# Last chunk's output rows: squares of the first halves ahead, two half rows scaled by ScalarE and GpSimd, VectorE's closing order written out

## The reference, cut to what matters

```python
    x = x + merged @ w_o[l].astype(merged.dtype)
    return rmsnorm(x, final_g)

def rmsnorm(x, g, eps=NORM_EPS):
    xf = x.astype(jnp.float32)
    y = xf * lax.rsqrt(jnp.mean(xf * xf, axis=-1, keepdims=True) + eps)
    return (y * g.astype(jnp.float32)).astype(x.dtype)
```

## Time and profile before

| | us |
|---|---|
| median of 3 runs | 2284.22 (2283.36 to 2284.63) |
| the profiled execution | 2282.93 |
| its span, first to last instruction | 2281.1 |
| TensorE busy | 2257.2 (99% of the span) |
| VectorE busy | 1426.0 (63%) |
| ScalarE busy | 756.0 (33%) |
| GpSimd busy | 232.8 (10%) |

### The profile page before, as it was taken

The page is one execution under the profiler, slowest core; times in us unless marked ns, Lnnn a source line. Parts: engine busy times, 40 slices in busy tenths (PEclk is TensorE's granted clock), DMA queues, the critical chain, the costliest instruction groups (busy, mean ns, idle before and its releaser), DMA issues.

```text
span 2281.1 us, 29046 instructions
## 1 busy us (share of the span) xinstructions
PE 2257.2 (99%) x10822; PEld 1832.9 (80%) x10822; DVE 1426.0 (63%) x2706; ACT 756.0 (33%) x1610; POOL 232.8 (10%) x186
## 2 busy tenths in 40 slices
PE   7999999999999999999999999999999999999998
PEld 6888888878888888888788788888877787788886
DVE  4767667764666665564557667665556657677752
ACT  4333332342333331032344344102135455441121
POOL 3544400100000000010000000001000000000010
PEclk9999999999999999999999999999999999999999
DMA  8877788798566665566755565556765555545555
GB/s 315 288 265 265 270 289 290 273 342 321 166 203 183 181 175 183 190 254 238 263 185 170 166 199 156 169 196 239 257 258 144 179 161 168 156 136 183 187 193 201
DMA packets 99339, 493.53 MB, mean 216 GB/s; under 512 B 15360, under 2 KB 18304, under 8 KB 54144
## 3 DMA queue, kind: packets, MB, share of 16 engines
q1 hardware_dynamic: 90464, 488.90, 63.8%
q10 hardware_dynamic: 8736, 2.78, 0.6%
HBM read 378.37 MB, written 113.27 MB: 216 GB/s over the span
## 4 chain that ended last, share of the span: by engine, by line
PE 96%; DVE 2%; DMA 1%; issue 1%; ACT 0%; SPq 0%; DVEq 0%; ACTq 0%
PE PJ L769 75%; PE SC L828 6%; PE SC L860 5%; PE TB L869 3%; PE OB L893 1%; PE OB L894 1%; PE OB L828 1%; PE PJ L828 1%; PE OB L896 1%; PE OB L895 1%; PE TB L904 0%; DMA Wraw<-w_stream 0%; DMA PX<-x_t 0%; PE TB L920 0%; PE SC L769 0%
## 5 line engine op out<-in xcount | busy, mean ns | idle before, releaser
L769 PE MATMUL PJ<-hT,Wp 128*128 128x512 f32 x6480 | 1571.4, 394 | 0.5 <-DVE PX L1632 0.5
L769 PEld LDWEIGHTS PJ<-hT,Wp 128*128 128x128 f32 x6480 | 1189.5, 188 | 254.0 <-issue 17.7
L1552 DVE SCALAR_TENSOR_TENSOR ACCS<-UA,col,ACCS 128x512 f32<-128x512 f32 x464 | 350.7, 798 | 0.4
L1066 ACT ACTIVATE PX<-SC,negm 128x512 f32<-128x512 f32 (+3 forms) x320 | 196.2, 623 | 145.5 <-DVE negm L1381 143.6
L1426 DVE TENSOR_TENSOR ZA<-TB,ZA 128x512 fp32r<-128x512 f32 (+1 forms) x144 | 95.1, 660 | 177.0 <-ACT ZA L1086 176.0
L1381 DVE TENSOR_REDUCE negm<-SC 128x2 f32<-128x1024 f32 (+3 forms) x160 | 169.0, 1061 | 40.3 <-PE SC L860 37.6
L1086 ACT ACTIVATE ZA<-TB 128x512 fp32r<-128x512 f32 (+1 forms) x144 | 82.6, 574 | 321.8 <-PE TB L869 321.8
L1137 ACT ACTIVATE TG<-PJ,col 128x512 f32<-128x512 f32 x64 | 44.1, 690 | 351.2 <-PE PJ L769 351.2
L1419 DVE SCALAR_TENSOR_TENSOR PX<-PX,sc 128x512 f32<-128x512 f32 (+3 forms) x160 | 108.0, 695 | 51.0 <-ACT PX L1077 50.8
L828 PE MATMUL SC<-Wp,KM 128*128 128x512 f32 x384 | 121.5, 389 | 0.0
L1077 ACT ACTIVATE PX<-PX,sc 128x512 f32<-128x512 f32 (+3 forms) x160 | 98.9, 655 | 64.9 <-DVE sc L1408 44.6
(11 more groups left out here) (192 smaller groups left out, 2037.4 us busy)
## 6 DMA issues: line engine op xcount, KB each, us to landing
Wp<-split_weights SPq DMA_DIRECT2D x264, 1024.0 KB, 4.8
split_weights<-Wp SPq DMA_DIRECT2D x88, 1024.0 KB, 4.9
Wraw<-w_stream SPq DMA_DIRECT2D x88, 512.0 KB, 5.9
KM<-keys SPq DMA_DIRECT2D x24, 512.0 KB, 5.9
VM<-values SPq DMA_DIRECT2D x24, 512.0 KB, 6.5
PX<-x SPq DMA_DIRECT2D x16, 512.0 KB, 7.6
out<-PX SPq DMA_DIRECT2D x16, 512.0 KB, 10.6
keys<-KM SPq DMA_DIRECT2D x12, 512.0 KB, 9.5
```

The costliest lines, as they stand in the source:

```text
L769: mm = pe.matmul(pj(c, r)[:, :], wt, rhs[:, 1 if q == 1 else 0, k, :], start=(n == 0), stop=(n == 3 * ktiles - 1))
L1066: a = act.activation(probs(c, h, t, j, m)[:, 0:w], SC[k][:, m, 0:w], ACT.Exp, bias=negm[:, t % 2, j, m:m + 1], accum_out=lsum[:, t % 2, j, ...
L1552: a = dve.scalar_tensor_tensor(out=acc, in0=src, scalar=col[:, n:n + 1], in1=acc, op0=ALU.mult, op1=ALU.add)
```

## The change

Only the last chunk is touched. ScalarE squares the first halves of the four rows ahead, while TensorE works on half 1, into `xst[:, 0, t]`; after the end of the projection it squares only the second halves, and VectorE adds the two sums, with one more 128x1 instruction ahead of each clamp. For rows 0 and 1, VectorE scales only the second half. The first half is multiplied by the factor on ScalarE (`end_scale`) and by `ffull` on GpSimd (`end_half`), and the stores of these two rows wait for both. VectorE's order at the end is written out, and so are ScalarE's and GpSimd's.

```diff
             def store_rows(c, t):
                 sp.wait_ge(row_ready, NT * c + t + 1)
+                if c == NCHUNK - 1 and t < 2:
+                    sp.wait_ge(half_ready, t + 1)
...
+            def half_square(t):
+                act.wait_ge(fin_freed, 8 * (NCHUNK - 1) + t + 1)
+                wait(act, half_squared, t)
+                if t == 0:
+                    act.wait_ge(rsq_done, NT * (NCHUNK - 1))
+                act.activation(junk[:, 0:CHUNK], xres[:, t, 0:CHUNK], ACT.Square, accum_out=xst[:, 0, t:t + 1]
+                               ).then_inc(half_squared, 1)
...
+                        if c == NCHUNK - 1 and p == FIN_AT + 26 + t:
+                            half_square(t)
...
-            for t in range(NT):
-                row_square(NCHUNK - 1, t)
+            def end_square(t):
+                act.wait_ge(fin_freed, 8 * (NCHUNK - 1) + NT + t + 1)
+                act.wait_ge(rsq_done, NT * (NCHUNK - 1) + t)
+                if t == 0:
+                    act.wait_ge(half_squared, NT)
+                act.activation(junk[:, 0:CHUNK], xres[:, t, CHUNK:], ACT.Square, accum_out=rst[:, 0, t:t + 1]).then_inc(rsq_done, 1)
+
+            def end_scale(t):
+                act.wait_ge(scale_ready, t + 1)
+                act.activation(xres[:, t, 0:CHUNK], xres[:, t, 0:CHUNK], ACT.Copy, scale=rst[:, 5, t:t + 1]).then_inc(half_scaled, 1)
+
+            end_square(0)
+            end_square(1)
+            end_square(2)
+            end_scale(0)
+            end_square(3)
+            end_scale(1)
...
-            for t in range(NT):
-                row_power(NCHUNK - 1, t)
+            def end_half(t):
+                pool.wait_ge(half_scaled, t + 1)
+                pool.tensor_tensor(xres[:, t, 0:CHUNK], xres[:, t, 0:CHUNK], ffull[:, 0:CHUNK], ALU.mult).then_inc(half_ready, 1)
+
+            row_power(NCHUNK - 1, 0)
+            row_power(NCHUNK - 1, 1)
+            end_half(0)
+            row_power(NCHUNK - 1, 2)
+            row_power(NCHUNK - 1, 3)
+            end_half(1)
...
-            for n in range(NT + 2):
-                if n < NT:
-                    add_rows(NCHUNK - 1, 1, n)
-                if n > 0 and n <= NT:
-                    row_clamp(NCHUNK - 1, n - 1)
-                if n > 1:
-                    row_scale(NCHUNK - 1, n - 2)
+            def end_clamp(t):
+                dve.wait_ge(rsq_done, NT * (NCHUNK - 1) + t + 1)
+                dve.wait_ge(half_squared, t + 1)
+                step(dve.tensor_tensor(rst[:, 0, t:t + 1], rst[:, 0, t:t + 1], xst[:, 0, t:t + 1], ALU.add))
+                clamp(rst, t, rvar_ready)
+
+            def end_rows(t):
+                n = NT * (NCHUNK - 1) + t
+                if t == 0:
+                    dve.wait_ge(f_loaded, 16 * NCHUNK)
+                dve.wait_ge(rpow_done, n + 1)
+                dve.wait_ge(rvar_ready, n + 1)
+                dve.tensor_tensor(rst[:, 5, t:t + 1], rst[:, 4, t:t + 1], rst[:, 3, t:t + 1], ALU.mult).then_inc(scale_ready, 1)
+                dve.wait_ge(scale_ready, t + 1)
+                first = CHUNK if t < 2 else 0
+                dve.scalar_tensor_tensor(out=xres[:, t, first:], in0=xres[:, t, first:], scalar=rst[:, 5, t:t + 1],
+                                         in1=ffull[:, first:], op0=ALU.mult, op1=ALU.mult).then_inc(row_ready, 1)
+
+            add_rows(NCHUNK - 1, 1, 0)
+            add_rows(NCHUNK - 1, 1, 1)
+            end_clamp(0)
+            add_rows(NCHUNK - 1, 1, 2)
+            end_clamp(1)
+            end_rows(0)
+            add_rows(NCHUNK - 1, 1, 3)
+            end_clamp(2)
+            end_rows(1)
+            end_clamp(3)
+            end_rows(2)
+            end_rows(3)
```

More of the change, by code:

```diff
@@ L542, in build @@
             sem("rsq_done"), sem("rvar_ready"), sem("rpow_done"), sem("row_ready"))
+        half_squared, scale_ready, half_scaled, half_ready = (
+            sem("half_squared"), sem("scale_ready"), sem("half_scaled"), sem("half_ready"))
         const_pool = sem("const_pool")
```

## The result

The changed kernel takes 2286.61 us (median of 22 runs, 2285.37 to 2288.25) against 2283.86 us for the kernel before (22 runs, 2282.78 to 2284.84) measured beside it: 2.75 us more, a ratio of 1.0012 (95% interval 1.0007 to 1.0018). That is within the 0.2% that was set as no change, and on the slow side of it. The interval, +1.6 to +4.1 us, holds the forecast (+2.57; 2286.8 us) and also rival D (+3.95); which of them it was, the profile has to tell.

The account below looks back on a forecast made before the run. VectorE's queue, then the last store, bound the end. Row 3's scaling: -0.66 + 0.91 + 1.09 = +1.34 us; with three stores in a row the span's end moves +2.57: 2284.22 + 2.57 = 2286.8 us, range 2283.5 to 2288.2.

Parts of the forecast that it names:

- rival D: At row 2's scaling VectorE wins the SBUF access and GpSimd's second half row comes later: +3.95 us, 2288.2 us; chance 0.10.
- What bounds: Behind the last matmul, VectorE's queue and then the last store set the end, not ScalarE's squares; 9.5 us cap any gain.
- The squares and sums: Half squares on ScalarE win nothing; VectorE's extra 128x1 sums cost three steps of 0.18 us on the path, +0.54 us.
- Half scaling: VectorE's scaling of rows 0 and 1 falls to 128x512, 0.60 us less each, a gain of 1.20 us.
- VectorE's own account: VectorE's gain from half scaling less its extra sums, before any hold: -1.20 + 0.54 = -0.66 us.
- The holds: GpSimd's two products hold VectorE at row 2's sum, +0.91 us, and at row 3's L1665, +1.09 us.
- The one that waits goes first: At SBUF access, the engine already waiting is served next: GpSimd's second product starts at 2276.78, ahead of row 3's L1665.
- The stores: Stores 2 and 3 queue behind store 1, which waits for GpSimd; three pass in a row at 1.28 us each.
- A: Rival: GpSimd's product doesn't hold VectorE, but the stores bunch at the end: +1.1 us, 2285.3 us; chance 0.15.
- B: Rival: VectorE is held but stores overlap, so the last row alone counts: +1.3 us, 2285.5 us; chance 0.12.
- C: Rival: neither holds nor bunched stores, VectorE's -0.66 us goes straight to the end: 2283.6 us; chance 0.08.
- D with a product of 1.9 us: Rival D with GpSimd's product at 1.9 us instead of 1.29: claimed over the bound of measurement; 0.04 left to slower.

## Why the prediction was right, point by point

- **What bounds.** VectorE's queue and then the last store, not ScalarE's squares: shown by the version with whole rows on VectorE, where all squares are halved and the tail is longer.
- **The squares and sums.** +0.54 us was forecast, +0.59 measured in row 3's readiness; a step is 0.19 and not 0.18 us. The half squares run from 2251.24 to 2254.42 and ScalarE is then idle for 14.51 us, so their cover held.
- **Half scaling.** The forecast took 0.60 us off for each of two rows; it is 0.53. The short scaling with these operands lasts 0.75 us and moves the next start by 0.67, where the row that was used, L1611 in the earlier trace rows, had 0.69. VectorE's own account is -0.48 and not -0.66 us. The mechanism held, this term was oversized. The row was not of the same kind: L1611 multiplies by a constant in the instruction (`scalar=1.0`), the scaling by a number per partition in SBUF. L1552 before, 464 instructions that read such a number (`col`), would have been the nearer row; L1613 has a constant again, like L1611:

```profile
L1552 DVE SCALAR_TENSOR_TENSOR ACCS<-UA,col,ACCS x464: 736/745/2964, 60.6 to 2160.8; 128x512 f32<-128x512 f32 x155
```
```profile
L1613 DVE SCALAR_TENSOR_TENSOR UC<-UC,SZA x16: 691/692/1690, 443.9 to 2195.4; 128x512 f32<-128x512 f32 x16
```

- **The holds.** Forecast 0.91 and 1.09 us, measured 0.70 (0.85 for 0.15) and 1.07 (1.22 for 0.15). The first is smaller because VectorE came 0.07 us later through its longer half scaling, GpSimd began 0.12 us earlier than forecast (the copy on ScalarE starts before the record of the accumulator's reading ends), and the product lasts 1.27 and not 1.29 us. The two errors, half scaling and first hold, nearly cancel: -0.48 + 0.70 + 1.07 = +1.29 (row 3's readiness moved by 1.28), against +1.34 forecast.
- **The one that waits goes first.** Rival D needed the opposite at row 2's scaling. The product was issued at 2276.73, in the middle of it, and passed ahead of L1830.
- **The stores.** Forecast +1.24 us over row 3's own lateness; 4.42 - 3.04 = 1.38 measured, and 1.27 comes back when row 2's store goes first. Three stores of 524 KB took 3.9 us, 3.84 forecast; the eight windows from 2279.5 to 2283.5 hold 377, 401, 393, 410, 418, 410, 401 and 336 GB/s, 1573 KB in all.
- **The rivals.** A (no hold) falls with the 0.85 and 1.22 us, B (stores overlap) with the store order, C (faster) with both. The version without the product is what C described, and its tail is 0.48 us shorter than before's.
- **The sum.** +2.57 us forecast, +2.66 in the profiles, +2.75 in the medians. That it comes so close is in part luck: 0.18 us too much gain on VectorE's own account, 0.23 us too much hold and 0.14 us too little for the stores nearly add up to nothing. The absolute 2286.8 is nearer still (2286.61) because the kernel before, measured beside it, ran 0.36 us under the median that the forecast was added to.
- **Slips in its text.** "Without it the second rival's does" should name the first, A: B has VectorE held. And D with a product of 1.9 us comes to 3.95 + 0.61 = 4.56 us, just under 0.2% of 2284.22 and not over it. Neither touches the forecast.

What the study leaves open: by what rule the waiting engine is served first is seen only at its effect, in the three profiles where the second product stood waiting and in the earlier trace rows; and why the last matmul starts within a range of 2.6 us from profile to profile wasn't looked into.

## What to carry to other kernels

Before handing VectorE's work to GpSimd, look at which of VectorE's instructions run beside it: here each with two SBUF tensors, be it 128x1, stood still beside a 128x512 product until that was all but done, so 1.27 us of help cost 0.7 to 1.1 us and saved 0.5. The 128x1 powers on GpSimd held nothing. Follow an offloaded piece to the in-order queue that waits for it: a store that waits late holds up stores whose rows are ready, and at a DMA share of 1.0 they can't make it up. If a multiplier such as `final_g` is known early, that product can be done ahead in an idle stretch rather than on a third engine at the end: here the tail was 1.05 us shorter for it, though the medians don't show a gain.

## What the runs showed of the hardware that was not expected

A 128x1 instruction with one tensor and a per-partition scalar operand isn't held by GpSimd's product (0.21 us beside it), while one with a second tensor of one element per partition is (0.85 and 1.22 us). That form has its price: 0.21 us and 0.24 to the next dependent instruction, against 0.15 and 0.19. The long instructions show the same 0.06 us: scalar_tensor_tensor, 128x512, all in SBUF, takes 0.69 us where the scalar is a constant (L1611 in the earlier trace rows, L1613) and 0.75 where it is a number per partition read from SBUF (L1552, and L1833 in the changed kernel). That is a comparison of lines that differ in their tensors too; no run changed the scalar of a long one alone.
